# Expert gate and up weights as half the rows by 1024 columns, two column groups at a time

## What is computed

```python
def swiglu(x, w_gate_up, w_down):
    g, u = jnp.split(x @ w_gate_up, 2, axis=-1)
    return (jax.nn.silu(g) * u) @ w_down

def moe_swiglu(xn, router_w, w_gate_up, w_down):
    ...
    for e in range(N_EXPERTS):
        out = out + combine[:, e:e + 1] * swiglu(xf, w_gate_up[e], w_down[e])
```

## Time and profile before

| | |
|---|---|
| median of 3 runs | 2243.08 us |
| the profiled execution, and its span | 2245.08 us, 2243.0 us |
| instructions | 28065 |
| expert weights of gate and up: DMAs, size, to landing | 224, 1024 KB, 8.6 us |
| expert weights of down: DMAs, size, to landing | 112, 1024 KB, 9.6 us |

### The profile page before, as it was taken

How to read it: one execution, slowest core, us unless ns; L and a number is a source line. 1 busy time by engine, 2 the same in 40 slices (tenths; PEclk the granted TensorE clock), 3 DMA queues, 4 the chain that set the end, 5 groups by cost and what they waited for, 6 DMA issues and landing times.

```text
span 2243.0 us, 28065 instructions
## 1 busy us (share of the span) xinstructions
PE 2193.6 (98%) x11072; PEld 1826.8 (81%) x11072; DVE 1586.5 (71%) x1334; ACT 1313.8 (59%) x1138; POOL 35.2 (2%) x56
## 2 busy tenths in 40 slices
PE   7999999999998999999999999999999999999998
PEld 6877788887776888888888888888888998898986
DVE  5565555465656888888888888898887657575664
ACT  5454544445545776676777767676676554456542
POOL 3100000000000000000000000000000000000000
PEclk9999999999998999999999999999999999999999
DMA  8554565554537999999999899999996544455442
GB/s 274 166 171 141 200 204 179 185 180 149 183 128 264 335 372 327 371 336 362 337 375 363 330 379 329 370 326 373 337 363 227 194 136 142 159 174 170 131 151 75
DMA packets 246121, 559.17 MB, mean 249 GB/s; under 512 B 11816, under 2 KB 14000, under 8 KB 245776
## 3 DMA queue, kind: packets, MB, share of 16 engines
q1 hardware_dynamic: 241920, 545.36, 68.2%
q0 software_dynamic: 3552, 10.93, 1.6%
q10 hardware_dynamic: 560, 1.64, 0.2%
HBM read 556.83 MB, written 1.06 MB: 249 GB/s over the span
## 4 chain that ended last, share of the span: by engine, by line
PE 94%; DVE 2%; ACT 2%; DMA 1%; issue 0%; DVEq 0%; ACTq 0%
PE bank L856 32%; PE bank L1125 9%; PE bank L1126 9%; PE bank L1129 9%; PE bank L862 8%; PE bank L1163 5%; PE bank L1158 5%; PE bank L1156 5%; PE bank L1019 3%; PE bank L903 3%; PE bank L1094 1%; DMA ring<-w_in 1%; DVE raw_low L2055 1%; ACT top L1569 1%; PE bank L1186 0%
## 5 line engine op out<-in xcount | busy, mean ns | idle before, releaser
L2422 DVE TENSOR_TENSOR w_low<-ring,w_high 128x4096 fp32r<-128x4096 f32 x168 | 739.6, 4420 | 55.8 <-ACT w_high L1780 54.2
L1780 ACT ACTIVATE w_high<-ring 128x4096 fp32r<-128x4096 f32 x168 | 610.7, 3635 | 240.6 <-DMA ring<-moe_w_down 94.8
L2055 DVE TENSOR_TENSOR raw_low<-ring,top 128x2048 fp32r<-128x2048 f32 x175 | 391.6, 2264 | 170.5 <-ACT top L1569 168.7
L1569 ACT ACTIVATE top<-ring 128x2048 fp32r<-128x2048 f32 x175 | 326.2, 1892 | 127.4 <-DMA ring<-w_in 59.5
L856 PE MATMUL bank<-top,xT_high 128*128 128x512 f32 (+1 forms) x928 | 358.5, 390 | 5.7 <-ACT top L1569 3.2
L1125 PE MATMUL bank<-w_high,xg_high 128*128 128x512 f32 x896 | 357.6, 399 | 1.7 <-DVE xg_low L2399 1.7
L1126 PE MATMUL bank<-w_high,xg_low 128*128 128x512 f32 x896 | 351.6, 392 | 0.0
L856 PE MATMUL bank<-top,xT_low 128*128 128x512 f32 (+1 forms) x928 | 348.8, 380 | 0.0
L1129 PE MATMUL bank<-w_low,xg_high 128*128 128x512 f32 x896 | 224.5, 392 | 0.0
L856 PE MATMUL bank<-raw_low,xT_high 128*128 128x512 f32 (+1 forms) x928 | 223.4, 379 | 0.0
L856 PEld LDWEIGHTS bank<-top,xT_high 128*128 128x128 f32 x928 | 175.3, 189 | 42.8 <-issue 9.0
(11 more groups left out here) (353 smaller groups left out, 2563.2 us busy)
## 6 DMA issues: line engine op xcount, KB each, us to landing
ring<-moe_w_gate_up SPq DMA_DIRECT2D x224, 1024.0 KB, 8.6
ring<-moe_w_down SPq DMA_DIRECT2D x112, 1024.0 KB, 9.6
ring<-w_in SPq DMA_DIRECT2D x108, 1024.0 KB, 5.2
ring<-w_out SPq DMA_DIRECT2D x24, 1024.0 KB, 4.9
ring<-ffn_w_gate_up SPq DMA_DIRECT2D x22, 1024.0 KB, 5.2
ring<-ffn_w_down SPq DMA_DIRECT2D x11, 1024.0 KB, 4.9
ring<-w_mem_kv SPq DMA_DIRECT2D x8, 1024.0 KB, 5.1
ring<-w_branch_attn SPq DMA_DIRECT2D x4, 1024.0 KB, 5.0
```

The lines of the kernel that those rows point to most:

```text
L1569: act.activation(top_view(half), raw_view(half), ACT.Copy).then_inc(top_in, 1)
L1780: act.activation(high_slot(k), ring[:, ring_r.slot(names[k]), :], ACT.Copy).then_inc(w_high_in[r], 1)
L2055: dve.tensor_tensor(raw_view(half, raw_low), raw_view(half), top_view(half).bitcast(F32), ALU.subtract).then_inc(raw_low_in, 1)
L2422: dve.tensor_tensor(w_low[:, slot, :], ring[:, slot, :], high_slot(k).bitcast(F32), ALU.subtract).then_inc(w_low_in[r], 1)
```

## The change

The gate and up tiles 0 to 11 become `TG` and `TU`: half of the rows (512) by 1024 columns. Four of them, `TG j 0`, `TG j 1`, `TU j 0`, `TU j 1`, carry the two gate and two up column groups 2j and 2j + 1. The seventh group keeps its old tiles 12 and 13. The number, size and order of the slots is as before. `up_wide` works on two banks at once; both are complete after the second of two tiles. What stood between two tiles (scatter, `ST`, the transposes) stands between the two halves, the transposes in pairs of groups. The order on ACT and DVE, and the banks, follow.

```diff
@@ -125,6 +125,7 @@
         order, held, s = [], set(), self.next
         if offsets is not None:
             order = [(s + k) % self.n for k in offsets]
+            s = (order[-1] + 1) % self.n
         for name in names[len(order):]:
             while s in held:
                 s = (s + 1) % self.n
@@ -177,8 +178,9 @@
 
 def expert_tiles(r):
     w = []
-    for j in range(EX_PAIRS):
-        w += [("EG", r, j), ("EU", r, j)]
+    for j in range(EX_PAIRS // 2):
+        w += [("TG", r, j, 0), ("TG", r, j, 1), ("TU", r, j, 0), ("TU", r, j, 1)]
+    w += [("EG", r, EX_PAIRS - 1), ("EU", r, EX_PAIRS - 1)]
     return w + [("ED", r, k) for k in range(EX_CH // 4)]
 
 
@@ -195,6 +197,12 @@
             out.append(turn)
             turn = (turn + 1) % (NSLOT - 1)
     return out
+
+
+def expert_banks():
+
+    count = len(expert_jobs("m"))
+    return [k % NBANK for k in range(count - 3)] + [6, 7, 3]
 
 
 def norm_jobs(*tag, blocks=range(TB)):
@@ -253,10 +261,13 @@
 
 
 def expert_jobs(r):
-    j = [("GX", r, 0), ("GX", r, 1), ("EG", r, 0)] + [("SC", r, b, n) for b in range(TB) for n in range(2)] + [("EU", r, 0), ("ST", r)]
-    for p in range(1, EX_PAIRS):
-        j += [("EG", r, p), ("ET", r, p - 1), ("EU", r, p)]
-    j += [("Y", r, 0), ("Y", r, 1), ("ET", r, EX_PAIRS - 1)]
+    j = [("GX", r, 0), ("GX", r, 1), ("EG", r, 0), ("EG", r, 1)]
+    j += [("SC", r, b, n) for b in range(TB) for n in range(2)] + [("EU", r, 0), ("EU", r, 1), ("ST", r)]
+    for p in range(2, EX_PAIRS - 1, 2):
+        j += [("EG", r, p), ("EG", r, p + 1), ("ET", r, p - 2), ("ET", r, p - 1), ("EU", r, p), ("EU", r, p + 1)]
+    last = EX_PAIRS - 1
+    j += [("EG", r, last), ("ET", r, last - 2), ("ET", r, last - 1), ("EU", r, last)]
+    j += [("Y", r, 0), ("Y", r, 1), ("ET", r, last)]
     return j
 
 
@@ -759,6 +772,9 @@
             if kind in ("EG", "EU"):
                 a = name[2] * WIDE + D_EXP * (kind == "EU")
                 return KC, WIDE, parts(t["moe_w_gate_up"][0, e, :, a:a + WIDE], KC)
+            if kind in ("TG", "TU"):
+                a = name[2] * D + D_EXP * (kind == "TU")
+                return 4, D, parts(t["moe_w_gate_up"][0, e, name[3] * WIDE:(name[3] + 1) * WIDE, a:a + D], 4)
             return 4, D, parts(t["moe_w_down"][0, e, name[2] * WIDE:(name[2] + 1) * WIDE, :], 4)
 
         block = ctx.enter_context(nc.Block())
@@ -1116,10 +1132,32 @@
                         slot = (tiles_f if r == "f" else tiles).slot(expert_tiles(r)[t])
                         return w_low[:, slot, :].rearrange("p (k n) -> p k n", n=n)
 
+                    def up_wide(kind, j, between):
+                        jobs = [(kind, r, 2 * j + n) for n in range(2)]
+                        o = [begin(job, e) for job in jobs]
+                        for hf in range(2):
+                            t = 4 * j + 2 * (kind == "EU") + hf
+                            w = high(t, 4, D)
+                            for c in range(4):
+                                for x, first in ((xg_high, hf + c == 0), (xg_low, False)):
+                                    for n in range(2):
+                                        pe.matmul(o[n][:, :], x[:, 4 * hf + c, :], w[:, c, n * WIDE:(n + 1) * WIDE],
+                                                  start=first, stop=False)
+                            w = low(t, 4, D)
+                            for n in range(2):
+                                for c in range(4):
+                                    mm = pe.matmul(o[n][:, :], xg_high[:, 4 * hf + c, :], w[:, c, n * WIDE:(n + 1) * WIDE],
+                                                   start=False, stop=hf == 1 and c == 3)
+                                if hf:
+                                    mm.then_inc(*end(jobs[n]))
+                            if not hf:
+                                mm.then_inc(*tile_end(("T" + kind[1], r, j, 0)))
+                                between()
+
                     def up(kind, p):
                         job = (kind, r, p)
                         o = begin(job, e)
-                        t = EG(p) if kind == "EG" else EU(p)
+                        t = EG if kind == "EG" else EU
                         w = high(t, KC, WIDE)
                         for c in range(KC):
                             pe.matmul(o[:, :], xg_high[:, c, :], w[:, c, :], start=c == 0, stop=False)
@@ -1133,16 +1171,23 @@
                         pe.wait_ge(*drained(("EU", r, p), e))
                         turn(("ET", r, p), [hid_e[:, p % 2, k * P:(k + 1) * P] for k in range(4)], e)
 
-                    up("EG", 0)
-                    for n in range(2):
-                        pe.wait_ge(*drained_last(("Y", r, n), e))
-                    scatter(("SC", r), e)
-                    up("EU", 0)
-                    turn(("ST", r), [sel[:, b, :] for b in range(TB)], e)
-                    for p in range(1, EX_PAIRS):
-                        up("EG", p)
-                        turn_hidden(p - 1)
-                        up("EU", p)
+                    def scatter_last():
+                        for n in range(2):
+                            pe.wait_ge(*drained_last(("Y", r, n), e))
+                        scatter(("SC", r), e)
+
+                    def turn_pair(j):
+                        for n in range(2):
+                            turn_hidden(2 * j + n)
+
+                    up_wide("EG", 0, scatter_last)
+                    up_wide("EU", 0, lambda: turn(("ST", r), [sel[:, b, :] for b in range(TB)], e))
+                    for j in range(1, EX_PAIRS // 2):
+                        up_wide("EG", j, lambda: turn_pair(j - 1))
+                        up_wide("EU", j, lambda: None)
+                    up("EG", EX_PAIRS - 1)
+                    turn_pair(EX_PAIRS // 2 - 1)
+                    up("EU", EX_PAIRS - 1)
                     acc = [begin(("Y", r, n), e) for n in range(2)]
                     for k in range(EX_PAIRS):
                         pe.wait_ge(*drained(("ET", r, k), e))
@@ -1787,33 +1832,42 @@
                         act.activation(flat(hid_high[:, 4 * p:4 * p + 4, :]), out_of(("ET", r, p))[:, :],
                                        ACT.Copy).then_inc(hid_high_in[r], 1)
 
-                    for p in range(EX_PAIRS):
-                        high(2 * p + 2, e)
+                    def silu(p):
                         if p >= 2:
                             act.wait_ge(*full(("ET", r, p - 2), e))
                         silu_gate(hid_e[:, p % 2, :], ("EG", r, p), WIDE, e)
-                        if p:
-                            hidden_high(p - 1)
-                        high(2 * p + 3, e)
+
+                    high(2, e)
+                    high(3, e)
+                    for j in range(EX_PAIRS // 2):
+                        high(4 * j + 4, e)
+                        for n in range(2):
+                            silu(2 * j + n)
+                        for k in range(5, 8):
+                            high(4 * j + k, e)
+                        if j == EX_PAIRS // 2 - 1:
+                            silu(EX_PAIRS - 1)
+                        for n in range(2):
+                            hidden_high(2 * j + n)
                     high(ED(2), e)
                     hidden_high(EX_PAIRS - 1)
                     for k in range(3, EX_PAIRS):
                         high(ED(k), e)
                     if follows:
                         xg_split([("GX", r, 0), ("GX", r, 1)], e + 1)
-                        high(EG(0), e + 1)
-                        high(EU(0), e + 1)
+                        high(0, e + 1)
+                        high(1, e + 1)
                         output_high(r, e)
 
                 more = None
-                high(EG(0), 0)
+                high(0, 0)
                 if r == "m":
                     mem_turned(0)
                     act.wait_ge(rt_gap, 1)
                     act.activation(rt[:, 66:68], rt[:, 64:66], ACT.Exp).then_inc(rt_exp, 1)
                     mem_turned(1)
                 xg_split([("GX", r, 0), ("GX", r, 1)], 0)
-                high(EU(0), 0)
+                high(1, 0)
                 if r == "m":
                     act.wait_ge(flag_ready, 1)
                     more = act.value_load(flag_word)
@@ -2436,34 +2490,38 @@
                         dve.tensor_tensor(flat(hid_low[:, 4 * p:4 * p + 4, :]), out_of(("ET", r, p))[:, :], v,
                                           ALU.subtract).then_inc(*fr(("ET", r, p)))
 
-                    low(EU(0), e)
+                    low(1, e)
                     scattered(("SC", r), e)
-                    low(EG(1), e)
-                    gate_up(0)
+                    low(2, e)
                     dve.wait_ge(*full(("ST", r), e))
                     dve.tensor_copy(flat(selT), out_of(("ST", r))[:, 0:TB * P]).then_inc(*fr(("ST", r)))
                     if follows:
                         choose(e + 1, offset, signal, e)
                     else:
```

(29 more changed lines are left out.)

## The result

The changed kernel takes 2276.05 us (median of 4 runs, 2268.52 to 2276.42) against 2243.62 (4 runs of the kernel before): a ratio of 1.0135, 95% interval 1.0123 to 1.0147. It is 32 us slower; 2265 was forecast, with a range of 2256 to 2276. The median stands at the very top of that range (0.05 us past its rounded end), and 11 us above the forecast.

A forecast was written before the change was run, and what follows sets the result against it. PE, without a gap in the expert stage, was taken as the bound. Waits 19.7, transposes -1.9 and clock +4.7 us made +22.5 on the median 2243.1, forecast as 2265 us, range 2256 to 2276.

The forecast's parts named there:

- What bounds the stage: Expert stage: PE alone has no gap, so added PE work or waits count in full and earlier weights give nothing.
- The wait at tile 3: PE at tile 3's w_low matmuls waits for DVE's subtraction, held behind ST: 2.21 us an expert, 1.45 in the last.
- The wait for ST's bank: PE's ST transposes wait until Silu 0 has read EG 0's bank: 0.39 us in each of seven experts.
- Sum of both waits: PE's waits for DVE's tile 3 subtraction and for the bank ST takes over, all experts: +19.7 us.
- The clock: PE's 2.05 us idle before tile 3 may bring 1.2 GHz, 1.58 us each: 0 to 12.6 us, +4.7 taken.
- three of eight: Count of experts in which the clock was taken to fall behind PE's idle time at tile 3: +4.7 us.
- the clock falls in every expert: Rival: 1.2 GHz level behind the tile 3 wait in all eight experts, 2273.5 us; chance 0.11.
- the stop of 1.64 us: PE's stop ahead of 257.00 us in the profile before, read as one that brought no clock change.
- Transposes in pairs: PE, each expert: three of six changes to transposes and back go, 0.08 us each, -1.9 us in all.
- Matmuls: Wide tiles on PE: same count, repeated operand loaded at the same price, no change; bounds -3.7 and +2 us.
- Sum: Whole kernel: 19.7 - 1.9 + 4.7 = +22.5 us, added to the median 2243.1, giving 2265.
- What is late next: DVE's and ACT's work behind tile 3's subtraction: PE waits for none of it, costed at nothing.

The follow-up runs named there:

- both repairs: Changed kernel with DVE's subtraction for tile 3 ahead of the wait for ST, and ST in the first scatter job's bank; 2243.97 us, ratio 0.9989 to 1.0007.
- this wait alone: Changed kernel with ST in the bank of the first scatter job in place of EG 0's; 2267.4 us, ratio 1.0092 to 1.0123.
- three kernels: The changed kernel (2276.05 us), the same with ST in the first scatter job's bank (2267.4), and the kernel before with ST's transposes behind tile 2 (2264.4).
- longer idle time: Changed kernel with two more selT copies on DVE, each waited for, ahead of choose; 2285.0 us, ratio 1.0168 to 1.0202.

## Why the prediction was right, and where its sizes were off

The mechanism was right: two new waits, at the places named and of the lengths named, and a clock that sometimes falls behind the longer one. That the median still lies at the top of the range is in part luck: the upper end was made with eight clock changes at the waits, and five reach it only together with 5 us of other terms that the sum had too low or left out.

- **What bounds the stage.** Right: in the variants with a wait, each us that PE waited came back in the length of the expert, and a 6% slower transfer did not.
- **The wait at tile 3.** Forecast 2.21 us an expert. The expert went from 124.83 (both repairs) to 127.17 (this wait alone): 2.34. The idle time was forecast as 2.05 and is 2.05; most of the rest is in the eight `w_low` matmuls behind it, which take 2.11 us in an expert without a clock change (from 864.31) where others take 2.00. The last expert's idle time was shorter, as forecast: 1.34 us, a wait of some 1.6 with the same addition. In all 7 x 2.34 + 1.6 = 18 us.
- **The wait for ST's bank.** Forecast 0.39 in seven experts, measured 0.36 (127.53 against 127.17).
- **Sum of both waits.** Forecast 19.7, measured 20.5.
- **The clock.** The term that was most mis-sized. Price right (1.58 forecast, 1.57 between the two lengths of an expert), count wrong: I took three of eight, the profile has five, 7.8 us in place of 4.7. The three were no more than a guess between two rows, and the rows were read for more than they hold: each stop had been seen once. Over twelve profiles the stop of 2.2 us brought the low clock in six, and the stop of 1.64 us that "changed nothing" brought it in the changed kernel, 1.81 us long there. The same idle time of 2.05 us gave five, three and two changes in three kernels, one profile each. One of the four runs of the changed kernel took 2268.5 at a mean clock of 0.994 where the others had 0.989 or 0.990; its 7.7 us less are what five changes cost, but its trace was not taken. What decides whether a stop brings a change stays open. The experiments show only how the count goes with the length: at 1.1 us of idle time none of eight, at 2.05 us ten of 21 (three kernels, seven experts each), at 3.0 us all seven. The shorter stop of the last expert brought none in the three kernels (1.34 us) and one in the kernel with longer idle time (2.27 us). The rival "the clock falls in every expert" was nearer to the time than the forecast (2273.5 against 2276.05), though not true. The Trainium skill does not say that every stop brings the clock down; that all eight would fall "by it alone" was my reading of it, and five, three and two did.
- **Transposes in pairs.** Forecast -1.9 us; by the expert lengths a change costs 0.03, so the pairs bring 8 x 3 x 0.03 = 0.7 at most. In the trace eight transposes take 0.79 us from first start to the next matmul, four took 0.36: nearly in proportion. My 0.08 was the small difference of two numbers read to 0.01, with a slope from only two points.
- **Matmuls.** Forecast 0 with bounds of -3.7 and +2. The order costs 8 x 0.25 = 2.0 us, at the upper bound. With both repairs an expert is only 0.10 us longer than before, so 0.15 comes back elsewhere; the pairs explain at most 0.09 of it.
- **Sum.** For the profiled execution 20.5 + 7.8 + 8 x 0.10 (wide tiles with their transposes and order) = 29.1 of 31.2 us of span. The other 2.1 us are outside the forecast: 1.0 lies ahead of the experts (the first gather starts at 700.62, before at 699.67 us), with the clock change at 258 us that the profile before does not have, and about 1 is in the first expert, with the one at 708.6. So the 8.7 us that the forecast of 22.5 is short of 31.2 are 3.1 for the count of clock changes at the waits, 2.7 for transposes and matmuls (-1.9 forecast, +0.8 measured), 0.8 for the waits, and these 2.1.
- **What is late next.** Right: PE waited at no other tile, in the changed kernel and in all variants.

## What to carry to other kernels

When the piece of work between two tiles is moved, ask for each engine what stands behind its wait for that piece; here two transposes that take PE 0.2 us, one tile later, cost 2.3 us an expert, because the next tile's subtraction stood behind them on DVE. Where one engine is busy all the time, rearranging what feeds it (longer rows, fewer changes) brings nothing, and any new wait comes in full, and in this kernel from about 2 us of idle time on it often came with 1.6 us more for the clock. What one profile shows of the clock behind a stop is one draw: look at the same stop in several executions before a count is forecast from it. A move of a consumer to a bank whose last reader has itself moved is a second wait that the diff does not show.

## What the runs showed of the hardware

A stop of PE of 2.05 us in a stretch of otherwise unbroken work can bring the 1.2 GHz level for 3.4 us, at 1.57 us each (10 of 21 stops, in three kernels); a stop of 1.1 us did so at none of eight experts, one of 3.0 us at all seven, in one profile each. One and the same stop of 2.2 us behind the experts did it in six of twelve executions. The Trainium skill, "TensorE: Matmul & The Clock Gate", Part 1, has activity release a throttled clock, and idleness bring the throttled state back; the runs agree that the low level follows stops, and show that at 2 us not each stop brings it. Two matmuls in a row with the same stationary operand, in two banks, are not faster than with operands in turn and one bank at a time, but 0.02 us per 16 slower (124.83 against 124.58 us an expert); which of the two does it is not shown.
